# The values of the decode items move to GpSimd's DMA queue, and the layer loop is written out

## The chip, the cores and the metric

The kernel runs on one core of one Trainium2 chip. Its time is the device time of one execution in microseconds (us); three runs of the kernel before gave 2197.28, 2205.12 and 2205.92, median 2205.12. TensorE (PE), VectorE (DVE), ScalarE (ACT), GpSimd (POOL) and SyncE (SP) each have a queue of instructions, and meet at semaphores. SyncE and GpSimd issue the transfers; all transfers share the core's 16 DMA engines.

## What is computed

One inference step of a two-layer decoder trunk, for a prompt of 256 tokens and for 8 decode sequences of 8 tokens each, 320 tokens together. Each layer is, in order:

```
x = LN(a*x + 0.5*SwiGLU(x))                        # FFN 1, inner width 2816
q,k,v ... = x @ w_in                               # one projection for three mixers
o_a = retention(...); o_b = dilated window attention(...); o_c = differential attention(...)
x = LN(a*x + concat(o_a, o_b, o_c) @ w_out)
x = LN(a*x + cross_attention(x, 256 memory tokens) @ w_xo)
x = LN(a*x + 0.5*SwiGLU(x))                        # FFN 2
```

For the decode sequences the keys and values of the past lie in caches in HBM: the differential attention's in pages of 128 tokens found through a page table (8 pages per sequence, 1024 past tokens), the window's as 768 gathered rows per sequence, the memory's as 256 rows per sequence. All is float32; a product is made of three matmuls on operands split into a high and a low part.

## The kernel before

**Stages.** A layer runs FFN 1, the projections, the mixer attention, retention, the output projection with the memory projections, the cross attention and its output, FFN 2. Weights come in slots of 128 x 2048 floats (or 1408 for the FFN's second product) through a ring of four slots: GpSimd's queue (line 497 on) does nothing but wait, for each slot in order, until TensorE has used up the slot four before, and fetch it. The mixing part has 32 slots of two halves each; the 16 slots up to and including the output projection's (H_OUT) carry halves 0 to 31, and the last of these is fetched when the projections have ended, since it takes the ring place of their last slot.

**Decode items.** The attention is a list of items (MIXER and CROSS, at the top). Decode items take two sequences at a time: four differential items (diff_dec), four window items (win_dec), four cross items (cross_dec); prompt items stand between them. TensorE (attention, line 855) does for each item i: scores of item i+1, transposes of item i, the value product of item i (values; line 811 for differential and window items, 832 for cross items). The mixer's order is diff_dec 0, four window prompt items, diff_dec 1, 2, 3, win_dec 0, 1, 2, one prompt item, win_dec 3, three prompt items.

**The cache buffers.** One SBUF tensor, cache, has four parts: two for the keys of the two sequences of one decode item, two for the values. It lies where the FFN's split weights lie, so nothing of it can be fetched until the FFN is done. The keys of item g+1 may be fetched when the scores of item g have ended (s_psum), its values when the value product of item g has ended (o_psum, or xv_psum in the cross part).

**SyncE's queue** issues all of this in one written order, together with the outputs: keys and values of diff_dec 0 as soon as FFN 1 is done; keys 1; outputs of the projections; the retention state; values 1; keys 2; keys 3; values 2; window keys 0; values 3; then keys and values of the window items in turn; keys and values of cross item 0. Later come the memory input, cross keys 1, and in turn cross keys g and cross values g-1, values 3, and behind them the outputs mk and mv (lines 483 and 485). A differential item is 2 x 8 pages for the keys and as many for the values (pages, line 397), one transfer of 128 x 256 floats each; the page's number is read from the table in SBUF into a register (page_numbers, line 387), ahead of the wait that releases the fetch. A window or cross item is two transfers for the keys and two for the values (pair, line 419).

**The layer loop** is a loop in the instruction streams of all five engines, with the layer number l in a register; the value that a wait compares with is l times a constant plus a constant (Signal.upto).

Of the kernel before, what the change touches and what calls it, by code (L numbers as in the profile page):

```python
# [39 lines left out]
L = 2  # L40
PAST, PAGE = 1024, 128
NPG = PAST // PAGE
# [5 lines left out]
WK = 768  # L48
# [13 lines left out]
FFN_SLOTS = NF + 2 * KD  # L62
# [43 lines left out]
def build(nc, a, o):  # L106
    ctx = ExitStack()
    with ctx:
# [238 lines left out]
        def wait_apart(eng, name, awaited, value):  # L347


            eng.wait_ge(awaited, value)  # L350
            eng.sem_inc(passed[name], 1)
# [13 lines left out]
        def _(sp):  # L365
# [17 lines left out]
            sp.wait_ge(const_in, 16 * len(CONSTS))  # L383
            with sp.Fori(0, L) as l:
                def page_numbers(g):
# [7 lines left out]
                def pages(numbers, what, ready, slot0):  # L393
                    for b2 in range(2):
                        for pg in range(NPG):
                            src = a[what][bass.ds(numbers[b2][pg], 1), bass.ds(l, 1)].rearrange("a b p c -> (a b p) c")
                            sp.dma_start(cache[:, slot0 + b2, 256 * pg:256 * pg + 256], src).then_inc(ready[b2].sem, 16)  # L397

                def after(kind, g):

                    return ITEMS.index((kind, g)) + 1
# [6 lines left out]

                def diff_values(numbers, before):
                    if before:  # L410
                        wait_apart(sp, "sp", o_psum.sem, o_psum.upto(l, before))
                    pages(numbers, "dv", v_ready, 2)

                def pair(name, used, before, g, ready, slot0, n):
# [12 lines left out]

                def win_values(g):
                    pair("wv", o_psum, g + 8, g, v_ready, 2, 2 * WK)

                def cross_keys(g, before):
                    pair("ck", s_psum, before, g, k_ready, 0, 2048)

                def cross_values(g, used, before):
                    pair("cv", used, before, g, v_ready, 2, 2048)

# [12 lines left out]
                diff_keys(numbers[0], 0)  # L449
                diff_values(numbers[0], 0)  # L450
                numbers += [page_numbers(1), page_numbers(2)]
                diff_keys(numbers[1], after("diff_dec", 0))
                outputs_of_projections()
                sp.dma_start(view(s_dec, [[1, 2048]]), layer_of(a["state"], l)).then_inc(st_in.sem, 16)
                diff_values(numbers[1], after("diff_dec", 0))
                diff_keys(numbers[2], after("diff_dec", 1))

                numbers.append(page_numbers(3))
                diff_keys(numbers[3], after("diff_dec", 2))
                diff_values(numbers[2], after("diff_dec", 1))  # L460
                win_keys(0)
                diff_values(numbers[3], after("diff_dec", 2))
                with sp.Fori(1, 4) as g:
                    win_keys(g)
                    win_values(g - 1)
                win_values(3)
                cross_keys(0, after("win_dec", 3))
                cross_values(0, o_psum, after("win_dec", 3))
                wait_apart(sp, "sp", st_act.sem, st_act.upto(l, 1))
# [8 lines left out]
                with sp.Fori(2, 4) as g:  # L478
                    cross_keys(g, g + (len(MIXER) + 1))
                    cross_values(g - 1, xv_psum, g - 1)  # L480
                cross_values(3, xv_psum, 3)
                sp.wait_ge(mk_act.sem, mk_act.upto(l, 8))
# [12 lines left out]
        @block.gpsimd  # L495
        def _(pool):
            pool.wait_ge(brow_out, 16)
            with pool.Fori(0, L) as l:
                def load(name, r, at, idx):

                    n = a[name].shape[2]
                    pool.wait_ge(w_used.sem, w_used.upto(l, 1 - RING) + at)
                    pool.dma_start(ring[:, r, 0:n],  # L503
                                   a[name][bass.ds(l * (a[name].shape[0] // L) + idx, 1)].rearrange("a p c -> (a p) c")
                                   ).then_inc(w_ready[r].sem, 16)

                pos, index = 0, {"w16": 0, "w11": 0}
                for name, count in SEGMENTS:
                    whole = count // RING * RING
                    with pool.Fori(0, whole // RING) as turn:  # L510
                        i = turn * RING
                        for j in range(RING):
                            load(name, (pos + j) % RING, i + (pos + j), i + (index[name] + j))
                    for j in range(whole, count):
                        load(name, (pos + j) % RING, pos + j, index[name] + j)
                    pos += count
                    index[name] += count


        @block.tensor  # L520
        def _(pe):
# [30 lines left out]

            with pe.Fori(0, L) as l:
                def three(out, wh, wl, xh, xl, first, last):
# [426 lines left out]
        def _(act):  # L981
# [7 lines left out]

            with act.Fori(0, L) as l:  # L990
                def high_weights(f, s, add=0):
# [185 lines left out]
        def _(dve):  # L1177
# [51 lines left out]
            dve.wait_ge(const_in, 16 * len(CONSTS))  # L1229
            with dve.Fori(0, L) as l:  # L1230
                step = [0]
# [572 lines left out]
```

## Time and profile before

| | |
|---|---|
| median of three runs | 2205.12 us |
| the profiled execution's own time | 2202.35 us |
| its span, first to last instruction | 2200.7 us |
| TensorE busy | 1912.7 us, 87% of the span |
| VectorE, ScalarE busy | 947.4 us (43%), 665.2 us (30%) |
| GpSimd busy | 114.6 us, 216 slot fetches |
| mean granted TensorE clock | 0.912 of full speed |
| TensorE busy and clock from 395 to 550 us (mixer attention, layer 0) | 100.76 of 155 us, clock 0.82 |
| the same from 1470 to 1630 us (layer 1) | 107.41 of 160 us, clock 0.78 |
| TensorE busy and clock from 720 to 815 us (cross attention, layer 0) | 73.67 of 95 us, clock 0.89 |

Times in rows are in microseconds from the span's start. A row of a timeline gives start, duration, engine, line, operation, operands and count, and in brackets how long the engine had stood idle and what ended that. Adjacent equal instructions are merged into one row, with their count; the duration is then from the first's start to the last's end. SPq is SyncE's own queue, and a DMA row of it is the time of issuing, not of moving the data.

### The profile page before, as it was taken

The numbers are of one execution on the slowest core, as the hardware profiler recorded it, in microseconds if no ns is written. First come the engines' busy times: TensorE is split into PE (matmuls) and PEld (weight loads), VectorE is DVE, ScalarE is ACT, GpSimd is POOL, SyncE is SP. The second block draws the span as 40 slices with busy tenths as digits, with TensorE's granted clock in tenths as the row PEclk, the third lists the DMA queues.
The fourth block names the chain that finished last, engine by engine and source line by source line (L and its number), as shares of the span: only waits on it lengthen the run. The fifth ranks groups of instructions, "written<-read, shape, count | busy, mean of one in ns | idle before, by whom it ended". The sixth has DMA issues, their size and how long they took to land.

```text
span 2200.7 us, 30802 instructions
## 1 busy us (share of the span) xinstructions
PE 1912.7 (87%) x11798; PEld 1670.3 (76%) x11798; DVE 947.4 (43%) x1514; ACT 665.2 (30%) x905; POOL 114.6 (5%) x220
## 2 busy tenths in 40 slices
PE   4999999666898878999979999986688897889998
PEld 2999988334787567999979998963357774779997
DVE  3554354313554235554355435442135442455534
ACT  1332242212243123332243323321123330333323
POOL 0000100000000000000100000000000000000000
PEclk8999989887798988999979999998858998989998
DMA  5443453665143622443424436446622436124432
GB/s 167 153 144 125 151 192 134 199 207 214 49 145 115 230 96 96 148 142 130 164 85 142 141 131 207 143 138 199 237 106 87 146 117 266 58 96 152 140 131 79
DMA packets 84411, 319.29 MB, mean 145 GB/s; under 512 B 10106, under 2 KB 45146, under 8 KB 59210
## 3 DMA queue, kind: packets, MB, share of 16 engines
q0 software_dynamic: 31104, 205.53, 27.2%
q1 hardware_dynamic: 53194, 112.24, 14.6%
q8 instruction: 72, 1.18, 0.2%
q14 instruction: 41, 0.34, 0.0%
HBM read 306.95 MB, written 10.79 MB: 144 GB/s over the span
## 4 chain that ended last, share of the span: by engine, by line
PE 80%; DVE 6%; DMA 6%; issue 4%; SPq 3%; ACT 2%; DVEq 0%; ACTq 0%
PE ps L556 18%; PE ps L558 18%; PE ps L557 18%; PE ps L525 5%; PE ps L811 3%; PE ps L650 3%; PE ps L652 3%; PE ps L651 3%; SPq L397 2%; DMA cache<-in_ck 2%; PE ps L729 2%; DMA cache<-in_wv 1%; PE ps L755 1%; PE ps L832 1%; PE ps L840 1%
## 5 line engine op out<-in xcount | busy, mean ns | idle before, releaser
L556 PE MATMUL ps<-x_high,w_high 128*128 128x320 f32 x1408 | 439.1, 312 | 23.8 <-DVE w_low L1249 16.7
L557 PE MATMUL ps<-x_low,w_high 128*128 128x320 f32 x1408 | 438.1, 311 | 0.0
L558 PE MATMUL ps<-x_high,w_low 128*128 128x320 f32 x1408 | 437.9, 311 | 0.0
L1000 ACT ACTIVATE w_high<-ring 128x2048 fp32r<-128x2048 f32 (+1 forms) x152 | 256.7, 1690 | 490.8 <-PE ps L558 478.6
L1249 DVE TENSOR_TENSOR w_low<-ring,w_high 128x2048 fp32r<-128x2048 f32 (+1 forms) x152 | 305.5, 2011 | 158.5 <-ACT w_high L1000 158.2
L556 PEld LDWEIGHTS ps<-x_high,w_high 128*128 128x128 f32 x1408 | 267.2, 190 | 24.4 <-issue 24.4
L557 PEld LDWEIGHTS ps<-x_low,w_high 128*128 128x128 f32 x1408 | 267.3, 190 | 0.0
L558 PEld LDWEIGHTS ps<-x_high,w_low 128*128 128x128 f32 x1408 | 267.1, 190 | 0.0
L556 PE MATMUL ps<-h_high,w_high 128*128 128x320 f32 x704 | 219.9, 312 | 6.2 <-DVE h_low L1277 6.2
L503 POOL DMA_DIRECT2D ring<-in_w x216 | 114.4, 529 | 2048.0 <-PE ps L558 1846.9
L1256 DVE TENSOR_TENSOR m_low<-ring,m_high 128x1024 fp32r<-128x1024 f32 x112 | 137.0, 1224 | 193.0 <-ACT m_high L1043 192.9
L558 PE MATMUL ps<-h_high,w_low 128*128 128x320 f32 x704 | 217.5, 309 | 0.0
L557 PE MATMUL ps<-h_low,w_high 128*128 128x320 f32 x704 | 217.4, 309 | 0.0
L1043 ACT ACTIVATE m_high<-ring 128x1024 fp32r<-128x1024 f32 x112 | 118.3, 1060 | 292.9 <-PE ps L558 162.7
L1273 DVE TENSOR_TENSOR gate<-gate,ps 128x320 f32<-128x320 f32 x88 | 43.0, 488 | 273.2 <-PE ps L558 273.2
L556 PEld LDWEIGHTS ps<-h_high,w_high 128*128 128x128 f32 x704 | 132.2, 188 | 7.2 <-issue 7.2
L557 PEld LDWEIGHTS ps<-h_low,w_high 128*128 128x128 f32 x704 | 132.2, 188 | 0.0
L558 PEld LDWEIGHTS ps<-h_high,w_low 128*128 128x128 f32 x704 | 132.1, 188 | 0.0
L556 PE MATMUL ps<-x_high,m_high 128*128 128x320 f32 x384 | 125.6, 327 | 4.2 <-DVE x_low L1572 4.2
L557 PE MATMUL ps<-x_low,m_high 128*128 128x320 f32 x384 | 123.3, 321 | 0.0
L558 PE MATMUL ps<-x_high,m_low 128*128 128x320 f32 x384 | 122.9, 320 | 0.0
L525 PE MATMUL ps<-ident,tok 128*128 128x128 f32 (+1 forms) x228 | 68.3, 409 | 48.5 <-ACT tok L1057 31.5
(260 smaller groups left out, 2658.1 us busy)
## 6 DMA issues: line engine op xcount, KB each, us to landing
ring<-in_w POOLq DMA_DIRECT2D x152, 1024.0 KB, 5.1
ring<-in_w POOLq DMA_DIRECT2D x64, 704.0 KB, 4.3
cache<-in_dk SPq DMA_DIRECT2D x128, 128.0 KB, 2.2
cache<-in_dv SPq DMA_DIRECT2D x128, 128.0 KB, 2.5
cache<-in_ck SPq DMA_DIRECT2D x16, 1024.0 KB, 6.5
cache<-in_cv SPq DMA_DIRECT2D x16, 1024.0 KB, 7.0
cache<-in_wk SPq DMA_DIRECT2D x16, 768.0 KB, 6.3
cache<-in_wv SPq DMA_DIRECT2D x16, 768.0 KB, 4.9
```

What stands on the lines that cost most here:

```text
L503: pool.dma_start(ring[:, r, 0:n], a[name][bass.ds(l * (a[name].shape[0] // L) + idx, 1)].rearrange("a p c -> (a p) c")).then_inc(w_ready[r ...
L525: return nc.tensor.transpose(out, in_, ident[0:in_.shape[0], 0:in_.shape[0]])
L556: mm(out, wh, xh, start=first, stop=False)
L557: mm(out, wh, xl, start=False, stop=False)
L558: return mm(out, wl, xh, start=False, stop=last)
L650: mm(out, xh, wh[:, c], start=first, stop=False)
L651: mm(out, xh, wl[:, c], start=False, stop=False)
L652: last = mm(out, xl, wh[:, c], start=False, stop=end)
L1000: fn(w_high[:, pos % 2, 0:n], ring[:, pos % RING, 0:n], ACT.Copy).then_inc(hi_w.sem, 1)
L1043: fn(m_high[place][:, q % 2, :], ring[:, pos % RING, 1024 * (q % 2):1024 * (q % 2) + 1024], ACT.Copy)\
L1249: V.tensor_tensor(w_low[:, pos % 2, 0:n], ring[:, pos % RING, 0:n], w_high[:, pos % 2, 0:n].bitcast(F32), ALU.subtract).then_inc(lo_w.sem, 1)
L1256: V.tensor_tensor(m_low[place][:, q % 2, :], ring[:, pos % RING, 1024 * (q % 2):1024 * (q % 2) + 1024], m_high[place][:, q % 2, :].bitcast ...
```

## The change

GpSimd's queue fetches the values of all decode items, put between its weight slots: behind the last slot of the output projection come the values of the four differential items, of the four window items and of cross item 0, each behind the wait that releases the buffers; behind the last slot of the mixing part come the values of cross items 1 to 3. The page numbers are read on GpSimd, behind the wait, eight at a time. SyncE keeps the keys, the inputs and the outputs, in the order they had. The layer loop becomes a Python loop on all five engines, so that each engine's stream holds both layers one behind the other and the layer number is a constant. The inner loops stay loops.

```diff
-            with sp.Fori(0, L) as l:
+            for l in range(L):
...
                 diff_keys(numbers[0], 0)
-                diff_values(numbers[0], 0)
                 numbers += [page_numbers(1), page_numbers(2)]
                 diff_keys(numbers[1], after("diff_dec", 0))
                 outputs_of_projections()
                 sp.dma_start(view(s_dec, [[1, 2048]]), layer_of(a["state"], l)).then_inc(st_in.sem, 16)
-                diff_values(numbers[1], after("diff_dec", 0))
                 diff_keys(numbers[2], after("diff_dec", 1))
 
                 numbers.append(page_numbers(3))
                 diff_keys(numbers[3], after("diff_dec", 2))
-                diff_values(numbers[2], after("diff_dec", 1))
                 win_keys(0)
-                diff_values(numbers[3], after("diff_dec", 2))
                 with sp.Fori(1, 4) as g:
                     win_keys(g)
-                    win_values(g - 1)
-                win_values(3)
                 cross_keys(0, after("win_dec", 3))
-                cross_values(0, o_psum, after("win_dec", 3))
...
                 with sp.Fori(2, 4) as g:
                     cross_keys(g, g + (len(MIXER) + 1))
-                    cross_values(g - 1, xv_psum, g - 1)
-                cross_values(3, xv_psum, 3)
...
         def _(pool):
             pool.wait_ge(brow_out, 16)
-            with pool.Fori(0, L) as l:
+            for l in range(L):
...
+                def diff_values(g):
+                    if g:
+                        pool.wait_ge(o_psum.sem, o_psum.upto(l, after("diff_dec", g - 1)))
+                    else:
+                        pool.wait_ge(w_used.sem, w_used.upto(l, POS_FFN1 + FFN_SLOTS))
+                    for b2 in range(2):
+                        numbers = nc.values_load_multi_w_load_instructions(
+                            pt[0:1, g * (2 * NPG) + b2 * NPG:g * (2 * NPG) + b2 * NPG + NPG], [mybir.EngineType.Pool],
...
+                        for pg in range(NPG):
+                            src = a["dv"][bass.ds(numbers[pg], 1), l:l + 1].rearrange("a b p c -> (a b p) c")
+                            pool.dma_start(cache[:, 2 + b2, 256 * pg:256 * pg + 256], src).then_inc(v_ready[b2].sem, 16)
+
+                def pair_values(name, g, n):
+                    for b2 in range(2):
+                        src = a[name][l:l + 1, 2 * g + b2:2 * g + b2 + 1].rearrange("a b p c -> (a b p) c")
+                        pool.dma_start(cache[:, 2 + b2, 0:n], src).then_inc(v_ready[b2].sem, 16)
+
+                def mixer_values():
+                    for g in range(4):
+                        diff_values(g)
+                    for g in range(4):
+                        pool.wait_ge(o_psum.sem, o_psum.upto(l, after("win_dec", g - 1) if g else after("diff_dec", 3)))
+                        pair_values("wv", g, 2 * WK)
+                    pool.wait_ge(o_psum.sem, o_psum.upto(l, after("win_dec", 3)))
+                    pair_values("cv", 0, 2048)
+
+                def cross_values():
+                    for g in range(1, 4):
+                        pool.wait_ge(xv_psum.sem, xv_psum.upto(l, g))
+                        pair_values("cv", g, 2048)
+
+                HEAD = (H_MK + 1) // 2
                 pos, index = 0, {"w16": 0, "w11": 0}
-                for name, count in SEGMENTS:
+                for name, count, then in (("w16", 22, None), ("w11", 16, None), ("w16", HEAD, mixer_values),
+                                          ("w16", 32 - HEAD, cross_values), ("w16", 22, None), ("w11", 16, None)):
...
                     pos += count
                     index[name] += count
+                    if then:
+                        then()
...
-            with pe.Fori(0, L) as l:
+            for l in range(L):
...
-            with act.Fori(0, L) as l:
+            for l in range(L):
...
-            with dve.Fori(0, L) as l:
+            for l in range(L):
```

## Rows read from the trace of the kernel before

**Rows 1.** The page's part 4, the chain that ended last, by engine.

```profile
PE 80%; DVE 6%; DMA 6%; issue 4%; SPq 3%; ACT 2%; DVEq 0%; ACTq 0%
```

**Rows 2.** Waits of the whole run: us in total, times, longest.

```profile
PE ps L729 <- DMA cache<-in_dk: 27.3, 4, 9.2
...
PE ps L811 <- DMA cache<-in_wv: 20.0, 6, 4.5
```

**Rows 3.** SyncE's timeline, layer 0's values (the columns: see above).

```profile
294.97 7.50 SPq L397 DMA_DIRECT2D cache<-in_dv  x16
...
454.67 7.77 SPq L397 DMA_DIRECT2D cache<-in_dv  x16
...
471.90 7.45 SPq L397 DMA_DIRECT2D cache<-in_dv  x16
```

**Rows 4.** TensorE's timeline, layer 0, line 811: V0, end of V1, V2, V3.

```profile
408.24 5.35 PE L811 MATMUL ps<-cache,arena 128*64 128x256 f32 x32 [0.36 <-ACT arena L1100]
...
451.62 0.65 PE L811 MATMUL ps<-hid,arena 64*64 64x256 f32 x4
...
465.79 5.36 PE L811 MATMUL ps<-cache,arena 128*64 128x256 f32 x32 [0.90 <-DMA cache<-in_dv]
471.08 0.65 PE L811 MATMUL ps<-hid,arena 64*64 64x256 f32 x4
...
481.96 6.03 PE L811 MATMUL ps<-cache,arena 128*64 128x256 f32 x32 [4.26 <-DMA cache<-in_dv]
```

**Rows 5.** The chain in order of time, layer 0: start, us, what.

```profile
478.97 2.86 DMA cache<-in_dv
```

**Rows 6.** TensorE's timeline, layer 1, line 811, as Rows 4.

```profile
1482.85 5.64 PE L811 MATMUL ps<-cache,arena 128*64 128x256 f32 x32 [0.36 <-ACT arena L1100]
...
1526.72 0.65 PE L811 MATMUL ps<-hid,arena 64*64 64x256 f32 x4
...
1542.33 3.67 PE L811 MATMUL ps<-cache,arena 128*64 128x256 f32 x32 [0.36 <-ACT arena L1100]
1545.93 0.65 PE L811 MATMUL ps<-hid,arena 64*64 64x256 f32 x4
...
1556.80 6.21 PE L811 MATMUL ps<-cache,arena 128*64 128x256 f32 x32 [4.25 <-DMA cache<-in_dv]
```

**Rows 7.** GpSimd's timeline: kernel start, last output-projection slot of each layer.

```profile
15.22 0.53 POOL L503 DMA_DIRECT2D ring<-in_w  x1 [0.18 <-issue]
15.94 0.53 POOL L503 DMA_DIRECT2D ring<-in_w  x1 [0.18 <-issue]
...
394.33 0.53 POOL L503 DMA_DIRECT2D ring<-in_w  x1 [7.63 <-PE ps L652]
...
1467.22 0.53 POOL L503 DMA_DIRECT2D ring<-in_w  x1 [7.63 <-PE ps L652]
```

**Rows 8.** SyncE, line 387: duration in ns, min/median/max, first and last start.

```profile
L387 SPq TENSOR_LOAD <-pt x16: 518/524/1386, 37.9 to 1512.8; - x16
```

**Rows 9.** Timeline of GpSimd and VectorE in FFN 1, layer 0.

```profile
63.27 0.53 POOL L503 DMA_DIRECT2D ring<-in_w  x1 [6.46 <-PE ps L558]
63.30 0.33 DVE L1275 CAST h_high<-gate 128x320 f32 x1 [0.17 <-DVE gate L1273]
```

**Rows 10.** The chain in order of time, cross attention, layer 0.

```profile
729.23 6.82 DMA cache<-in_ck
...
770.98 8.58 DMA cache<-in_cv
```

**Rows 11.** SyncE's timeline, the output mk of layer 0.

```profile
771.41 0.38 SPq L483 DMA_DIRECT2D out_mk<-hid  x1
```

**Rows 12.** The chain at the layer's end, after VectorE's jump back (line 1230).

```profile
1110.53 3.61 issue
```

**Rows 13.** ScalarE's timeline at the layer's end.

```profile
1113.95 1.28 ACT L1000 ACT_TABLE_LOAD   x1 [2.62 <-issue]
```

**Rows 14.** TensorE's queue, line 614: duration in ns, min/median/max, first and last start.

```profile
L614 PEldq ALU_OP  x126: 32/32/32, 300.9 to 1918.5; - x126
```

More of the change, by code:

```diff
@@ L407, in diff_keys @@
                     pages(numbers, "dk", k_ready, 0)
[L409 to L412, printed above, removed]
                 def pair(name, used, before, g, ready, slot0, n):
@@ L426, in win_keys @@
                     pair("wk", s_psum, g + 8, g, k_ready, 0, 2 * WK)
-                def win_values(g):
-                    pair("wv", o_psum, g + 8, g, v_ready, 2, 2 * WK)
                 def cross_keys(g, before):
                     pair("ck", s_psum, before, g, k_ready, 0, 2048)
-                def cross_values(g, used, before):
-                    pair("cv", used, before, g, v_ready, 2, 2048)
                 def outputs_of_projections():
@@ L505, in load, with after @@
                                    ).then_inc(w_ready[r].sem, 16)
+                def after(kind, g):
+                    return ITEMS.index((kind, g)) + 1
+                def diff_values(g):
[6 more added lines that the diff above has]
+                            pt[0:1, g * (2 * NPG) + b2 * NPG:g * (2 * NPG) + b2 * NPG + NPG], [mybir.EngineType.Pool],
+                            min_val=0, max_val=a["dv"].shape[0] - 1,
+                            skip_runtime_bounds_check_because="a page table holds numbers of pages of its cache")[1]
+                        for pg in range(NPG):
+                            src = a["dv"][bass.ds(numbers[pg], 1), l:l + 1].rearrange("a b p c -> (a b p) c")
+                            pool.dma_start(cache[:, 2 + b2, 256 * pg:256 * pg + 256], src).then_inc(v_ready[b2].sem, 16)
```

## The prediction, made before the result was known

> **What bounds the kernel now.** I read the chain that ended last first [rows 1]: TensorE holds four fifths of it, transfers 6%, SyncE's queue 3%, and time in which an engine waited for nothing visible 4%. So the place to look is where TensorE stands still for a transfer. The whole-run waits [rows 2] name the keys of the differential items (27.3 us in 4 waits) and the values of the window items (20.0 us in 6). The values of the differential items, which the change touches most, show in TensorE's timeline instead. I call an item's value product V0, V1, V2, V3 (line 811, 32 matmuls on the cache and four on the new tokens). In layer 0, V2 waits 0.90 us and V3 4.26 us [rows 4]; in layer 1, V2 waits for ScalarE alone and V3 4.25 us [rows 6]. The values have one buffer pair, so item g+1 can be fetched only when Vg has ended: fetching is a serial step between two products, and what counts is the time from the end of Vg to the landing of the last of 16 pages.
>
> SyncE's timeline shows what its queue adds to that [rows 3]. V1 ended at 451.62 + 0.65 = 452.27, and values 2 began at 454.67, because SyncE was still issuing keys 3: a delay of 2.4 us, of which TensorE saw 0.90. V2 ended at 471.73 [rows 4] and values 3 began at 471.90: no queue in the way. The 16 issues ran to 478.97, and the last page landed 2.86 us later [rows 5], at 481.83. So an unhindered item on SyncE takes 10.1 us from release to landing. That is the number to beat.
>
> **The change part by part.**
>
> *Values on GpSimd, the pitch.* The last two of GpSimd's four back-to-back slot loads at the kernel's start stand 0.72 us apart (15.22, 15.94), each busy 0.53 [rows 7]. A page has 128 rows as a slot has, only shorter, so I expect the same pitch; SyncE's 16 value pages take 7.07 us for 15 steps, 0.47 each [rows 3, 5]. Bounds: 0.53 if only the busy time counts, 1.06 if two such times come one behind the other; I take 0.72, the nearest row. The page numbers were read ahead of the waits on SyncE; now they are read behind the wait, twice per item, 0.52 us each [rows 8]. From release to landing on GpSimd: 0.1 + 0.52 + 0.7 to the first issue (an estimate: one pitch), 15 x 0.72 = 10.8 to the last, 0.52 for the second read in the middle, landing 2.9 as on SyncE: 15.5 us against 10.1.
>
> The Trainium skill (Runtime: NRT & Kernel Launch, Instruction fetch mechanics) gives about 200 ns per register for a register load. Eight numbers would then cost 1.6 us; the trace has 0.52 for eight [rows 8], so the measurement decides. By the page the sum would be some 2.2 us per item higher, about 9 us over both layers.
>
> *Layer 0.* Values 0 were issued at 294.97, during the projections [rows 3]. Now they stand in GpSimd's queue behind the last slot load of the output weights, whose record is 394.33 [rows 7]: the reads begin near 394.9, so landing is 394.9 + 15.4 = 410.3, and V0 starts there instead of 408.24: +2.1. Values 1 have over 20 us: nothing. Values 2: V1 ends at 454.4, landing 469.9 against a start at 465.79: shift 4.1. Values 3: V2 ends at 475.8, landing 491.3 against 481.96: shift 9.3. Each of these waits ends last at its product, and the items behind are chained through the same buffers, so nothing makes it up.
>
> *Layer 1.* The slot record is 1467.22 [rows 7]: landing 1483.2 against 1482.85, +0.4. Values 2: V1 ends at 1527.37 + 0.4, landing 1543.3 against 1542.33: shift 1.0. Values 3: 1546.58 + 1.0 + 15.5 = 1563.1 against 1556.80: shift 6.3. Both layers: +15.6.
>
> *Window values.* Two transfers per item, three waits per layer [rows 2]. SyncE's first issue comes 0.17 us behind the release [rows 3, 4]; on GpSimd 0.7, and the second 0.1 to 0.15 later still: +0.6 each, +3.6 in all (0 to +6).
>
> *Memory values in the cross part.* Items 1 and 2 no longer stand behind keys, but the next keys end last there: 0. For item 3, GpSimd's later start costs 0.6. On the other side SyncE, now free of it, issues the two outputs (771.41 before [rows 11], right behind values 3) some 18 us earlier, so values 3 share the DMA engines with nothing: 8.58 us could fall to the 6.82 of the first keys [rows 10], -1.8. Net -1.2 per layer, -2.4 in all; between -5 and +4, as the outputs may instead hold up the last keys or values 2.
>
> *Keys alone on SyncE.* Keys are released by the score products and were issued at once before, so the 27.3 us of waits [rows 2] stay: 0. Window keys 0 stood behind values 2, but nobody waited for them.
>
> *Layer loop written out.* At the layer's end VectorE stood 3.61 us [rows 12] and ScalarE 2.62 [rows 13] for nothing but the jump back. Straight code needs no jump: the start of layer 1's first product moves up between 2.6 and 3.6; I take -3.1, once. The table load of 1.28 behind the jump may go too, but VectorE's own work then ends last.
>
> Waits in layer code also lose their computed values. TensorE's queue spends 32 ns on one, 126 times at line 614 [rows 14], 4.0 us in all, mostly under matmuls that already run; I take -1 for all such, bounds 0 and the whole of "issue" in [rows 1].
>
> *Sum.* 15.6 + 3.6 - 2.4 - 3.1 - 1 = +12.7. Against that, the written-out loop may also cheapen the address of each key page; two batches of 16 per layer lie on the path, so I allow -2. That leaves +10.7 on the profiled execution's own 2202.35 (span 2200.7), 2213. Its median counterpart is 2205.12, 2.8 higher, with runs from 2197.28 to 2205.92; I place the forecast for the median at 2215.
>
> **A rule against the change.** In FFN code GpSimd issues a slot load at 63.27 while VectorE casts from SBUF to SBUF at 63.30 [rows 9]; GpSimd's record is 0.53 long there too, like those of [rows 7]. The Trainium skill (SBUF — State Buffer, Two separate sides) says that GpSimd cannot write its descriptors while VectorE runs a copy in a two-port mode, so that a DMA from GpSimd seems blocked by it. The trace does not show which mode the cast runs in, but it shows no lengthening. If the rule bit here, it would do so where VectorE scales an item's probabilities, once per item; the sum would move towards the dear case below, and by the row it stays.
>
> **The rivals.**
>
> *GpSimd's pages are dear (slower, 2244).* Two busy times per page, pitch 1.06, release to landing 20.6. V0 +7.3 and +5.6, V2 to 14 and 11, V3 to about 24.5 and 21.5; with the other terms +42. For it: no row shows GpSimd issuing 16 transfers in a row or reading page numbers. Against: the four in a row at 0.72. Chance 0.14.
>
> *GpSimd's pages are cheap (not slower, 2201).* Pitch 0.53: release to landing 12.6. V0 lands at 407.4, no wait; values 2 land before 465.79 in layer 0; V3 +1.9 and +2.2. With half of the window term and the same gains about -1 to -2 on 2202.35. For it: busy is only 0.53. Against: the rest of the 0.72 was there at the kernel's start with nothing in the way. It decides from a pitch of about 0.6 down. Chance 0.24.
>
> *The written-out layers pay much more (faster, 2190).* If a quarter of "issue" in [rows 1], 4% of 2200.7 = 88 us, is sequencer work for the layer number, 22 us go, and even with the forecast's +10.7 the time falls to some 2191 of the profiled execution. For it: such operations stand in every engine's queue. Against: one is 32 ns, and the chain gives the queues themselves next to nothing apart from SyncE's. Chance 0.12.
>
> *The values' delay is hidden.* If the product order had slack, +0. The 4.26 and 4.25 us waits of V3 exclude it: they end last already. It has no chance of its own.
>
> **How the numbers follow.** Forecast (2206 to 2226) 0.50, dear 0.14, cheap 0.24, much more 0.12. The predicted time is 2215. The range 2194 to 2240 leaves out most of the fast case and the upper half of the dear one, about 2 in 10. A measurement can tell about 0.5%, 11 us: slower means over 2216, which takes nearly half of the forecast and all of the dear case, 0.40; faster means under 2194, the fast case and a little of the cheap one, 0.15; within, 0.45.
>
> **What would show it.** In the profile after: GpSimd's page issues 0.72 us apart and two number reads of 0.5 ahead of each eight (right) or 0.5 / 1.1 (rivals); V0 in layer 0 waiting for values near 2 us; V3 waiting over 9 us in both layers; the gap of 3.6 at the layer's end gone; the two memory outputs issued right behind the last keys. The prediction is wrong if V3's wait did not grow by about 5 us, or if the FFN stretches changed length.

## The result, and the profile after

The changed kernel takes 2239.66 us (median of 4 runs, 2237.28 to 2244.89); the kernel before, measured beside it, 2205.52. The ratio is 1.0165, interval 1.0132 to 1.0198: 36 us slower by the ratio and 34 by the medians, where the forecast for the median stood 10 us above the one of before. The profiled execution spans 2235.3 us (before 2200.7), at a granted TensorE clock of 0.903 (before 0.912).

The page's part 4 of after, the chain by engine, answers to [rows 1]:

```profile
PE 79%; DVE 7%; DMA 7%; issue 3%; ACT 2%; SPq 1%; POOL 0%; POOLq 0%; ACTq 0%; DVEq 0%
```

SyncE's queue has nearly left the chain (3% to 1%), and GpSimd's hasn't taken its place. What has grown is transfers: not the issuing, but the landing. TensorE's waits for them over the whole run (us in total, times, longest), as [rows 2]:

```profile
PE ps L752 <- DMA cache<-in_dk: 26.4, 4, 8.9
PE ps L834 <- DMA cache<-in_dv: 25.8, 4, 8.8
PE ps L834 <- DMA cache<-in_wv: 23.4, 6, 5.3
PE ps L778 <- DMA cache<-in_ck: 17.0, 6, 5.1
PE ps L855 <- DMA cache<-in_cv: 14.4, 4, 4.5
```

The same waits of before: dk 27.3, dv 9.4, wv 20.0, ck 11.1, cv 12.3. The growth is 16 us for the differential values, 3 for the window's, and 8 in the cross part, where the prediction had a gain.

GpSimd's timeline of after, layer 0, answers to [rows 7] (brackets: idle before). Line 483 is the last slot load ahead of the values, line 504 the value pages:

```profile
394.93 0.53 POOL L483 DMA_DIRECT2D ring<-in_w  x1 [7.63 <-PE ps L675]
396.58 4.63 POOL L504 DMA_DIRECT2D cache<-in_dv  x8 [1.12 <-issue]
401.86 4.63 POOL L504 DMA_DIRECT2D cache<-in_dv  x8 [0.65 <-issue]
...
457.39 4.63 POOL L504 DMA_DIRECT2D cache<-in_dv  x8 [28.17 <-issue]
462.97 4.63 POOL L504 DMA_DIRECT2D cache<-in_dv  x8 [0.96 <-issue]
480.66 4.63 POOL L504 DMA_DIRECT2D cache<-in_dv  x8 [13.06 <-issue]
485.93 1.71 POOL L504 DMA_DIRECT2D cache<-in_dv  x3 [0.64 <-issue]
488.99 2.89 POOL L504 DMA_DIRECT2D cache<-in_dv  x5 [1.35 <-issue]
```

Eight pages last 4.63 us, so a page starts (4.63 - 0.53) / 7 = 0.585 us after the one before; the forecast had 0.72. The gaps between the eights (0.65, 0.96 and 0.64) hold the second read of page numbers, 0.56 us each time in the chain of after. From the last issue to the landing, in the chain of waits of after, for values 0, 2 and 3 of layer 0 (start, us, what), as [rows 5]:

```profile
405.95 5.91 DMA cache<-in_dv
...
467.06 6.01 DMA cache<-in_dv
...
491.34 2.52 DMA cache<-in_dv
```

The forecast had 2.9 for all. Two of three are twice that. What lay beside them is in SyncE's timeline of after: keys 1 (first row), window keys (second; window keys 0 are the first two of its eight), and the memory outputs:

```profile
400.60 8.85 SPq L397 DMA_DIRECT2D cache<-in_dk  x16
...
465.26 50.48 SPq L414 DMA_DIRECT2D cache<-in_wk  x8
...
774.19 0.35 SPq L463 DMA_DIRECT2D out_mk<-hid  x1
774.59 0.64 SPq L465 DMA_DIRECT2D out_mv<-hid  x1
```

Before, window keys 0 stood behind values 2 in one queue. Now they start at 465.26, two microseconds ahead of the last page of values 2. Values 0, which before were fetched long ahead, now go beside keys 1. TensorE's value products V0, V2 and V3 of layer 0 and V3 of layer 1 in after answer to [rows 4, 6]:

```profile
412.00 5.50 PE L834 MATMUL ps<-cache,arena 128*64 128x256 f32 x32 [3.51 <-DMA cache<-in_dv]
...
473.21 5.62 PE L834 MATMUL ps<-cache,arena 128*64 128x256 f32 x32 [4.94 <-DMA cache<-in_dv]
493.99 5.47 PE L834 MATMUL ps<-cache,arena 128*64 128x256 f32 x32 [8.61 <-DMA cache<-in_dv]
...
1586.06 5.56 PE L834 MATMUL ps<-cache,arena 128*64 128x256 f32 x32 [8.78 <-DMA cache<-in_dv]
```

In the cross part, the chain of after, values 2 and 3 of layer 0 (before: 8.58 for values 3 [rows 10]):

```profile
778.03 14.75 DMA cache<-in_cv
...
799.88 7.79 DMA cache<-in_cv
```

and TensorE there, scores of item 3, V2 and V3:

```profile
782.00 6.49 PE L778 MATMUL ps<-cache,tok 128*32 128x256 f32 x32 [4.80 <-DMA cache<-in_ck]
792.92 6.15 PE L855 MATMUL ps<-cache,arena 128*32 128x512 f32 x16 [2.42 <-DMA cache<-in_cv]
807.82 5.53 PE L855 MATMUL ps<-cache,arena 128*32 128x512 f32 x16 [4.51 <-DMA cache<-in_cv]
```

To see where the time went I set the start of each matmul in after against the start of the same matmul in before. The difference stands still in the FFNs and moves at a few places. Where a stage is named, the row is one matmul within it, the same in both kernels:

| matmul | before | after | difference |
|---|---|---|---|
| V0, layer 0 | 408.24 | 412.00 | 3.8 (0.6 of it was there before V0) |
| V2 | 465.79 | 473.21 | 7.4 |
| V3 | 481.96 | 493.99 | 12.0 |
| values of window item 2 | 514.80 | 530.90 | 16.1 |
| memory projections | 635.27 | 656.12 | 20.9 |
| last transposes of layer 0 | 1102.33 | 1130.24 | 27.9 |
| first of layer 1 | 1119.66 | 1144.08 | 24.4 |
| V3, layer 1 | 1556.80 | 1586.06 | 29.3 |
| memory projections, layer 1 | 1720.36 | 1744.98 | 24.6 |
| output of the cross attention, layer 1 | 1896.04 | 1930.11 | 34.1 |
| end | 2200.7 | 2235.3 | 34.6 |

So the mixing parts cost 20 us up to the memory projections, 20.3 of it in layer 0 and 0.2 in layer 1, where the 4.9 that V3 had lost were gone by then. The cross parts cost 7.0 + 9.5 = 16.5, and the layer's edge gave 3.5 back.

### The profile page after: what moved, and what is told of

Same layout as the page of the kernel before. It is cut to its first block, busy times and chain, and to the rows that moved or that the text cites. A ratio compares the mean times of both kernels' runs of the same rounds, so it can differ in the third digit from the quotient of the medians.

```text
span 2235.3 us, 29464 instructions
## 1 busy us (share of the span) xinstructions
PE 1924.1 (86%) x11798; PEld 1674.9 (75%) x11798; DVE 948.1 (42%) x1514; ACT 662.6 (30%) x903; POOL 200.6 (9%) x380
## 4 chain that ended last, share of the span: by engine, by line
PE 79%; DVE 7%; DMA 7%; issue 3%; ACT 2%; SPq 1%; POOL 0%; POOLq 0%; ACTq 0%; DVEq 0%
PE ps L579 18%; PE ps L580 18%; PE ps L581 18%; PE ps L548 5%; PE ps L834 4%; PE ps L673 3%; PE ps L674 3%; PE ps L675 3%; DMA cache<-in_cv 2%; DMA cache<-in_wv 2%; PE ps L752 1%; DMA cache<-in_ck 1%; PE ps L855 1%; PE ps L778 1%; SPq L397 1%
## 5 line engine op out<-in xcount | busy, mean ns | idle before, releaser
L834 PE MATMUL ps<-cache,arena 128*64 128x256 f32 (+1 forms) x448 | 75.0, 506 | 52.0 <-DMA cache<-in_dv 25.8
```

Source lines behind the costliest of these rows:

```text
L834: last = mm(ps[w * b2:w * b2 + w, 7, 0:256], lhs, rhs, start=(k == 0), stop=(k == nk))
```

## The experiments

Ratios are to the kernel before in the same session, with 95% intervals. In the diffs, "..." stands for lines left out. Three theories were open: the memory outputs, which SyncE now reaches before the last values are asked for, take bandwidth from them (cross part); window keys, freed from their place behind the values, do the same to the pages of values 2 and 3 (mixing part); GpSimd's issuing behind each release is by itself too slow (mixing part).

**The outputs held back.** One wait on SyncE in the kernel after:

```diff
+                sp.wait_ge(xv_psum.sem, xv_psum.upto(l, 3))
                 sp.wait_ge(mk_act.sem, mk_act.upto(l, 8))
```

> The changed kernel, with one wait more on SyncE: the outputs mk and mv go out when the values of cross item 3 may be fetched, as in the kernel before. Theory O (the outputs, now issued right behind the last keys, share the DMA engines with keys 3 and values 2): the last keys wait 2 to 3 us again instead of 4.8, values 2 do not wait, values 3 wait 5 to 8 us; the two cross stretches give back 10 to 15 of the 17 us that they lost, total 2222 to 2230. Rival G (GpSimd's queue is itself the slower way for transfers of 1 MB): values 2 and 3 wait as long as in the changed kernel, total within 4 us of 2239.

Measured: 2233.40, ratio 1.0118 (1.0083 to 1.0153). The wait for values 2 is gone and keys 3 are waited for 3.41 us instead of 4.80, but the wait for values 3 is up to 9.2. The release of the outputs is also that of values 3, and SyncE is the quicker: its first output goes out 0.27 us ahead of the first of GpSimd's two transfers. The chain and SyncE's timeline of this kernel:

```profile
795.11 12.35 DMA cache<-in_cv
```

```profile
794.32 0.35 SPq L464 DMA_DIRECT2D out_mk<-hid  x1
794.72 0.43 SPq L466 DMA_DIRECT2D out_mv<-hid  x1
```

Part of the cost had only moved to the next item. The expectation had 5 to 8 us for this wait and 2222 to 2230 for the time, and missed both.

**The outputs last.** The same wait with 4 in place of 3, that is, behind the last value product:

```diff
+                sp.wait_ge(xv_psum.sem, xv_psum.upto(l, 4))
```

> As e1, but the outputs wait until the product on values 3 has ended, so that no key or value of a cross item shares the DMA engines with them. Theory O: values 3 land about 7.3 us after their first issue as keys 1 do, some 2 us sooner than in the kernel before; the cross stretches lose nothing against before, total 2218 to 2224. Rival G: within 4 us of 2239.

Measured: 2225.47, ratio 1.0078 (1.0055 to 1.0101). Values 3 land in 7.81 us (the same view), and the wait for cv falls from 14.4 to 8.4 us. The difference to before now grows by 0.5 us from the first scores of the cross part to FFN 2 in layer 0 (in after by 7.3) and by 3.3 in layer 1 (in after by 10.0): 13.5 us less in the traces. In time, against 1.0165, it is 0.0087, or 19 us, known to about 9, for one place in a queue. The time is 1 us above the expected 2218 to 2224. Of the 3.3 us that layer 1 still loses, 1.8 fall in the output projection, which runs at the lower clock for longer. Keys are also waited for longer, ck 14.4 us in all against 11.1 before.

```profile
792.25 7.81 DMA cache<-in_cv
```

**The other way round: before, with the outputs early.** No GpSimd in it. The outputs move in SyncE's queue of the kernel before, and the short inner loop over cross items 2 and 3 is written out for it:

```diff
+                cross_keys(3, 3 + (len(MIXER) + 1))
...
+                sp.dma_start(layer_of(o["mk"], l), ...)
...
+                sp.dma_start(layer_of(o["mv"], l), ...)
+                cross_values(2, xv_psum, 2)
                 cross_values(3, xv_psum, 3)
```

> The kernel before, all on SyncE's one queue, with the outputs mk and mv moved to behind keys 3 and ahead of values 2. Theory O: the outputs cost here too, values 2 and 3 wait for them, slower by 6 to 18 us over both layers, 2211 to 2223; keys 3 are ahead of them in the queue and wait no longer than before (2.7 us). Rival G: the outputs alone cost nothing, 2203 to 2208.

Measured: 2220.62, ratio 1.0049 (1.0023 to 1.0075). Values 2 land 14.64 us after their issue in the chain of this kernel, as in after (14.75):

```profile
765.82 14.64 DMA cache<-in_cv
```

The order alone makes the landing time, with no second queue. Both have keys 3 ahead of them too, but those are not the reason: with keys 3 ahead and the outputs held, the last of values 2 landed after 8.9 us in "outputs held back" and 8.7 in "outputs last". The wait for cv rose from 12.3 to 17.2 us, that for ck from 11.1 to 13.2. Keys 3 were waited for 4.51 us (before 2.73), where the expectation had no change: 2 MB issued right behind a transfer slow it as well. In time it costs 11 us here, against 19 in after; they are known to about 6 and 9 us, so that the two may be one.

**The written-out loop alone.** Before, with a Python loop in place of Fori on all five engines:

```diff
-            with sp.Fori(0, L) as l:
+            for l in range(L):
```

> The kernel before with only the layer loop written out on all five engines. Theory: the gap at the layer's end goes (3.6 us on VectorE) and hardly anything else, 3 to 5 us faster, 2200 to 2203. Rival (the layer number's arithmetic costs at every wait): 10 us or more faster, under 2196.

Measured: 2199.52, ratio 0.9977 (0.9952 to 1.0002). The layer's edge gives 3.5 us in the profile, as in after: TensorE stands 6.45 us ahead of layer 1's first product instead of 9.95. The wait for the differential keys falls from 27.3 to 23.9 us, and V3 waits 3.68 instead of 4.26 [rows 4]:

```profile
479.51 5.87 PE L811 MATMUL ps<-cache,arena 128*64 128x256 f32 x32 [3.68 <-DMA cache<-in_dv]
```

From here on the kernels carry "outputs last", so that only the mixing part is in question.

**Window keys held.** SyncE issues window keys 0 and 1 only when values 2 and 3 have landed:

```diff
-                win_keys(0)
-                with sp.Fori(1, 4) as g:
+                for s in range(2):
+                    for r in v_ready:
+                        sp.wait_ge(r.sem, r.upto(l, 16 * NPG * (3 + s)))
+                    win_keys(s)
+                with sp.Fori(2, 4) as g:
                     win_keys(g)
```

> e4 (values on GpSimd, outputs last) with the keys of window items 0 and 1 held on SyncE until the pages of values 2 and 3 have landed, so that these pages share the DMA engines with no keys. Theory C (contention from SyncE's freed queue, besides the serial issue): values 2 of layer 0 land 3 us behind their last issue instead of 6, V2's shift against the kernel before falls from about 5 to 2 us; V3 gains 0 to 1; the held keys may then be late by 0 to 3 us each. Total 0 to 4 us under e4. Rival S (only the serial issue of 16 pages and two reads behind the release costs): V2 and V3 start where they do in e4, total equal to e4 or up to 4 us above it, for the late keys.

Measured: 2214.39, ratio 1.0038 (1.0014 to 1.0061), 0.0040 below "outputs last", known to about 0.003: 9 us, where 0 to 4 were expected. The landing of values 2, first in the chain of "outputs last", then in the chain of this kernel, and TensorE's V2 and V3 of this kernel, layer 0:

```profile
466.54 6.02 DMA cache<-in_dv
```

```profile
465.18 2.57 DMA cache<-in_dv
```

```profile
467.89 5.36 PE L838 MATMUL ps<-cache,arena 128*64 128x256 f32 x32 [1.79 <-DMA cache<-in_dv]
...
488.25 5.83 PE L838 MATMUL ps<-cache,arena 128*64 128x256 f32 x32 [8.27 <-DMA cache<-in_dv]
```

Values 2 land in 2.57 instead of 6.02 and V2's wait falls from 5.10 to 1.79. A wait was added and the kernel became faster. V3's wait in layer 0 is nearly as long as in "outputs last" (8.85): there values 3 had landed in 2.75 already, and in after in 2.52.

**Page numbers read ahead.** "Outputs last", the numbers read ahead of the wait, and values 0 fetched behind the fourth slot of the mixing part, during the projections:

```diff
+                    ahead = page_numbers(g)
                     if g:
                         pool.wait_ge(o_psum.sem, ...)
...
+                                          ("w16", 4, first_values), ("w16", HEAD - 4, mixer_values),
```

> e4 with GpSimd's page numbers read ahead of the wait that releases the buffers, and values 0 fetched between the fourth and the fifth weight slot of the mixing part, as early as in the kernel before. Theory S: V0's shift of 3 us in layer 0 goes, V2 and V3 start 1.1 us sooner per item, in all 5 to 8 us under e4. Rival C: V0's 3 us go, and no more.

Measured: 2219.11 (eight runs from 2207.86 to 2222.93), ratio 1.0041 (1.0015 to 1.0068), 0.0037 below "outputs last", known to about 0.0035. V0 waits for nothing but its probabilities. V2 and V3 of layer 0, and ahead of them the landing of values 2 in the chain:

```profile
460.48 5.92 DMA cache<-in_dv
```

```profile
466.53 6.22 PE L843 MATMUL ps<-cache,arena 128*64 128x256 f32 x32 [3.57 <-DMA cache<-in_dv]
...
487.72 5.86 PE L843 MATMUL ps<-cache,arena 128*64 128x256 f32 x32 [8.42 <-DMA cache<-in_dv]
```

The landing of 5.9 is untouched: issue and landing are two costs.

**The pages back on SyncE.** "Outputs last" with the differential values at their old places in SyncE's queue; GpSimd keeps the window and memory values:

```diff
                 diff_keys(numbers[0], 0)
+                diff_values(numbers[0], 0)
...
-                    for g in range(4):
-                        diff_values(g)
```

> e4 with the values of the differential items back on SyncE, in the order of the kernel before; window and memory values stay on GpSimd. Theory: the page issue is what the mixing part lost, so V0, V2 and V3 come back to within 1 us of the kernel before; with the outputs last and the loop written out the kernel is 0 to 6 us faster than before, 2200 to 2208. Rival (two large queues beside each other cost by themselves, window values too): 2210 or more.

Measured: 2204.06, ratio 0.9983 (0.9959 to 1.0006). V2 waits for no transfer and V3 3.68, as in the loop alone (0.9977). So moving the window and memory values and putting the outputs last are together worth nothing that can be measured, and the whole rest, 0.0078 - (-0.0017) = 0.0095 or 21 us, is the pages'.

**All three mended.** The kernel after with outputs last, keys held and numbers ahead.

> The kernel after with three edits together, each run before by itself or with one other: mk and mv outputs behind cross values 3, window keys 0 and 1 held until values 2 and 3 have landed, page numbers read ahead of the waits with values 0 fetched in the projections. If the losses of the kernel after are separate things that add: V0 without a wait, release to landing of an item 16 x 0.585 + 2.6 = 12 us, so V2 waits under 1.5 and V3 5 to 6.5 us, and e4_outs_last's 2225 loses 11 (e5_keys_held) and 6 (e6_reads_ahead): 2205 to 2211, about the kernel before. Rival, the two edits work on the same microseconds, because the landing of a page hides its neighbours' slow issue: no better than the better of the two, 2213 to 2219. Rival, the lower granted clock of 550 to 725 us (0.80 against 0.86 before) is a loss of its own that stays: mixing waits as in the first case, time 2211 to 2216.

Measured: 2205.94, ratio 0.9997 (0.9977 to 1.0017). From "outputs last" (1.0078), the two edits took 0.0040 and 0.0037 by themselves; together 0.0081, so they add up as far as this can be told. V2 no longer waits for values; V3 of layer 0 and the differential values' whole wait:

```profile
481.66 5.79 PE L846 MATMUL ps<-cache,arena 128*64 128x256 f32 x32 [4.83 <-DMA cache<-in_dv]
```

4.83 us on GpSimd's queue against 4.26 on SyncE's [rows 4], and this hides part of the cost: TensorE first stands 2.74 us for the held window keys. From release (468.1) to landing (479.15 + 2.37) values 3 take 13.4 us, where SyncE took 10.1 and the expectation had 12. The time is within the expected 2205 to 2211, so the rival that a lower clock keeps part of the loss falls. It is not a tie on equal terms: this kernel has the written-out loop, and against the loop alone (0.9977) it stands 0.0020 or 4 us behind, less than can be told.

**The two sequences split.** A version from what was learnt: loop written out, outputs last, and for each differential item sequence 0's pages (keys and values) by SyncE and sequence 1's by GpSimd, numbers ahead; window and memory values on SyncE.

```diff
+                def keys(numbers, before):
+                    pool.wait_ge(s_psum.sem, s_psum.upto(l, before))
+                    pages(numbers, "dk", [None, pg_ready["k1"]], 1)
...
+                def values(numbers, before):
+                    pool.wait_ge(o_psum.sem, o_psum.upto(l, before))
+                    pages(numbers, "dv", [None, pg_ready["v1"]], 3)
```

> Another division: layer loop written out, outputs mk and mv last, and of each differential item sequence 0's 8 pages of keys and of values come from SyncE, sequence 1's from GpSimd, numbers read ahead; window and memory transfers all on SyncE as before. If the serial issue behind the release is what an item waits for, both keys 2, keys 3 and values 3 land about 4 us sooner: 11 us less wait per layer, 22 in all, and 5 to 7 more from loop and outputs, 2175 to 2186. Rival (the DMA engines' rate bounds the pages, 2 MB per item): half of that or less, 2190 to 2202.

Measured: 2187.15, ratio 0.9896 (0.9852 to 0.9941): faster than both kernels, and 1 us above the expected range. Against the loop alone it is 0.0081 or 18 us, known to about 11. Both queues issue eight pages at a time, so the wait for dk falls from 27.3 (23.9 with the loop alone) to 18.2 us. But V3 of layer 0 waits longer than before, and the chain and SyncE's timeline say why:

```profile
480.50 5.90 PE L866 MATMUL ps<-cache,arena 128*64 128x256 f32 x32 [7.69 <-DMA cache<-in_dv]
```

```profile
472.49 7.87 DMA cache<-in_dv
```

```profile
471.32 0.87 SPq L424 DMA_DIRECT2D cache<-in_wk  x2
```

SyncE is done with its eight pages sooner than GpSimd, and its window keys start 1.2 us ahead of GpSimd's last page.

**Split, with window keys held**, as above but for values 2 and 3 of this kernel.

> e8_split with one edit: SyncE issues window keys 0 only when values 2 have landed, and window keys 1 only when values 3 have landed. Contention theory: in e8_split the last page of values 3 landed 7.87 us after its issue, because window keys 1 were issued right behind it; held back, landing falls to about 2.6, the wait of V3 from 7.7 to 2.5 to 4 us in both layers, and the time from e8_split's 2187 to 2177 to 2184. Rival, the landing is slow because two queues write the two halves at once: landing stays near 8 and the time at 2185 to 2190. Second rival, the held window keys come late: a wait of TensorE for wk above 3 us in place of the wait for dv, time 2185 to 2192.

Measured: 2189.31, ratio 0.9913 (0.9877 to 0.9948): no better, where 2177 to 2184 was expected. TensorE's waits of this kernel:

```profile
PE ps L872 <- DMA cache<-in_wv: 20.9, 6, 5.2
...
PE ps L800 <- DMA cache<-in_wk: 8.3, 4, 3.1
...
PE ps L872 <- DMA cache<-in_dv: 0.5, 1, 0.5
```

The wait for dv went from 12.8 to 0.5, more than expected, and the one for wk from 2.1 to 8.3. V3 starts 7.8 us earlier (472.66 against 480.50), yet the end moves by 3 in the profile and not at all in the median. The second rival holds: the window keys are the next item's bound, and now they come late. Over all cache transfers the waits fell by 7.4 us in the profile, the span by 3.3, and the median by nothing that can be told; where the rest of the 7.4 went is open.

## Why the prediction was wrong

The direction was right, and the size was not: +36 where +10 stood. In the traces it is 34.6 us of span against a sum of 10.7. By its steps:

- **The failed step is "Memory values in the cross part".** It priced the freed outputs as a gain, -2.4, since values 3 would then share with nothing. Values 3 did land sooner, as the step said, though in 7.79 and not in 6.82 (before 8.58). But the outputs stood right behind keys 3 (774.19), as forecast too, and it was values 2 and keys 3 that met them: values 2 landed in 14.75. The step knew this danger as its upper bound ("the outputs may instead hold up the last keys or values 2") and ended it at +4; it is +16.5 over both layers in the traces, which is 19 of the 24 us that the sum fell short, and "outputs last" takes back 13.5 us in the traces and 19 in time. It had used the landing time of one item (8.58 with 2 MB of outputs behind it in the same queue) and not asked what the same 2 MB do ahead of it.
- *Pitch*: 0.585, not 0.72; the bounds of 0.53 and 1.06 held. *Reads*: 0.56 to 0.57 against 0.52 in the chain, the first one 0.78. *Landing*: 5.9 and 6.0 for values 0 and 2, not 2.9. The prediction said of window keys 0 that nobody waited for them; true, but they now compete with what is waited for. For values 2 "window keys held" shows this; that keys 1 do the same to values 0 is read from the timeline and wasn't tested. So, less the 0.6 us that were there before V0, V0's difference is 3.2 instead of 2.1, V2's 6.8 instead of 4.1, and V3's 11.4 instead of 9.3 in layer 0. In layer 1 V3's is 4.9 (29.3 less 24.4) instead of 6.3.
- *Both mixing parts together*: forecast 15.6 + 3.6 = 19.2, measured 20. That they agree is luck. The total hides a pitch too dear, a landing too cheap, and one thing with no price: in item 3 of layer 0 GpSimd stood 1.35 us ahead of the twelfth page. It also holds the changes of the clock below, +3 in layer 0 and -2.7 in layer 1. The wait for window values grew by 3.4, as forecast.
- *V3's wait*: forecast over 9 us, 8.61 and 8.78; about 5 more than before, 4.35 and 4.53.
- *Loop*: forecast -3.1, -1 and -2; the edge gave 3.5 here and alone, and the loop alone is 0.9977, -5 us with an interval from -11 to 0. Right as far as this can be told.
- *Rivals.* The dear case stood at 2244, 4 us from the result. Its mechanism, a pitch of 1.06, is refuted by the timeline. By the time alone the wrong theory would have been confirmed. The cheap case falls with the time and not with its mechanism: its pitch of 0.53 is nearer to the 0.585 than the forecast's 0.72, and by its own mark, a pitch of about 0.6 or less, it should have held. What it lacked is what the forecast lacked, the outputs and the slow landings. Much more falls with the time, and with the loop alone.
- *The rule against the change*, GpSimd blocked by VectorE's copies: seven of the eight groups of eight pages in layer 0 last 4.63 us to the hundredth (five are shown), among them two beside VectorE's scaling of an item's probabilities (456.91 and 480.18, 0.79 us each). In the broken group GpSimd stood from 487.64 to 488.99, and VectorE's last instruction before that ended at 483.82. So the rule is the cause neither of the size nor of that stop. For layer 1's stop of 2.26 us, beside which VectorE was at work, it is open.

What the Trainium skill says of this (DMA: Bandwidth & Descriptors, Issuing engines are not separate DMA queues) is that transfers started by sync and gpsimd run on the same 16 DMA engines and interleave. The traces agree: 7.81 us alone, 8.58 with the outputs behind in the same queue, 12.35 with them at the same time in the other queue. The Trainium skill goes on, in the same section, that a second issuing engine only saves issue time. Here it also took away an order, and that cost 0.0087 of the time.

One reading that I first had is withdrawn. In the window from 550 to 725 us the granted clock is 0.86 before and 0.80 after, which looks like a loss of its own. But after lags by 17 us there, and the same window holds more of the slow stretch. The same stretches of work, set by hand to whole microseconds, in before (the columns: window; us, then busy time and count of PE, PEld, DVE, ACT, POOL; clock, DMA share, GB/s):

```profile
530.00:568.00 38.00, 29.69 (x152) 22.38 (x149) 16.22 (x55) 8.34 (x37) 0.00 (x0) 0.58 0.16 58
568.00:636.00 68.00, 57.84 (x393) 52.70 (x393) 43.54 (x88) 23.00 (x38) 2.64 (x5) 0.90 0.30 106
...
1608.00:1652.00 44.00, 35.54 (x170) 25.75 (x171) 16.22 (x55) 10.28 (x47) 0.00 (x0) 0.54 0.19 71
```

and after:

```profile
547.00:587.00 40.00, 31.71 (x153) 23.93 (x150) 16.37 (x55) 8.45 (x37) 1.05 (x2) 0.54 0.15 55
587.00:657.00 70.00, 59.59 (x387) 54.33 (x386) 43.53 (x88) 22.93 (x38) 2.65 (x5) 0.87 0.31 106
...
1636.00:1678.00 42.00, 33.15 (x167) 24.06 (x168) 16.31 (x55) 10.67 (x47) 1.05 (x2) 0.57 0.21 82
```

The same work takes 2 + 2 us more in layer 0 at a slightly lower clock (most of what separates the window items' and the memory projections' rows of the table) and 2 less in layer 1 at a slightly higher one. The edge of it shows in the retention. There eight matmuls on the decode state (line 915, in after 938) take 1.97 us where the granted clock is 0.50 (1.2 GHz) and 1.09 where it is 1.00 (2.4 GHz). In layer 0 the first three such groups take 1.97, 1.97 and 1.82 us in after, and 1.09 each in before; in layer 1 it is before that has the long ones. The kernel with the loop alone, in which no value moved, has long ones in layer 0 as after has, and loses about the same 3 us there. So it moves by microseconds either way, and its share in layer 0 comes without any moved value.

**Left open.** Why GpSimd paused 1.35 us at one page: it did so at the same page of values 3 in after, "outputs held back", "outputs last" and "window keys held", for 1.73 us at that page where the numbers were read ahead, and for 1.33 at the fourth page in both split kernels. The timeline names no releaser, and VectorE stood idle beside it in the first four. In layer 1 a gap of 2.26 us stands inside values 1, where it costs nothing. Why the clock rises some microseconds later in layer 0 with the loop written out is open too.

## What to carry to other kernels

A queue that issues for several consumers is also a priority list: before moving a transfer off it, list what stood behind it, ask when that will now start, and what waited-for transfer it will meet on the shared DMA engines. Price a landing by rows that have the same bytes ahead of it, beside it or behind it, not by the nearest row of the same transfer. Bulk that nobody waits for (outputs) belongs behind the last thing that somebody waits for, if need be by a wait of its own; and splitting one item's pages over two queues shortens the serial issue, where moving all of them to the other queue only changed its owner, here to one with a longer pitch (0.585 for 0.47).

## What the runs showed that I had not expected

- A pair of memory values (2 MB) is complete 7.81 us after the issue of its second transfer when alone, 8.58 with 2 MB of outputs behind it in the same queue, and 12.35 with those issued 0.8 us and less ahead on the other queue. With keys 3 ahead it is 8.7 to 8.9, and with keys 3 and the outputs ahead 14.75 or 14.64, in either queue.
- The last of 16 pages of 128 KB lands 2.3 to 2.6 us after its issue with the window keys held, 2.9 and 3.6 in before, where two 768 KB transfers were issued 0.8 and 0.6 us behind it in the same queue, and 5.9 to 7.9 where those began 0.5 to 2.0 us ahead of it on the other queue. Beside the next item's key pages (values 0) it took 5.1 to 6.1.
- GpSimd's pitch for a page is 0.585 us; its reads of eight page numbers take 0.56 to 0.78 us each. For values 3 it is 1.2 us from the release to the first page (479.4 to 480.66).
- The edits' costs added up (0.0040 and 0.0037 alone, 0.0081 together, each known to about 0.003), though both act on the same chain of waits.
